# Products of constants in three norms of a two-layer block given up, TensorE waits there

## The reference

```python
def rmsnorm(x, g):
    xf = x.astype(jnp.float32)
    y = xf * lax.rsqrt(jnp.mean(xf * xf, axis=-1, keepdims=True) + EPS)
    return (y * g.astype(jnp.float32)).astype(x.dtype)
...
    for l in range(DEPTH):
        ...
        a_lat = rmsnorm(h, norm1_g[l]) * (1.0 + sc1) + sh1
        a_ctx = rmsnorm(z, norm1_g[l]) * (1.0 + csc1) + csh1
        o_ctx, o_lat = token_mixer(a_ctx, a_lat, ...)
        h = h + g1 * o_lat
        f_lat = rmsnorm(h, norm2_g[l]) * (1.0 + sc2) + sh2
        h = h + g2 * channel_mixer(l, f_lat, ...)
        if need_ctx:      # layer 0 only
            ...           # the same for the context tokens
    return rmsnorm(h, final_g)
```

## Time and profile before

| what | value |
|---|---|
| median of 3 executions | 1991.33 us |
| the profiled execution | 1993.04 us |
| its span, first to last instruction | 1991.3 us |
| TensorE busy | 1949.7 us, 98% of the span |
| TensorE loading weights | 1591.6 us, 80% |
| VectorE busy | 1558.4 us, 78% |
| ScalarE busy | 992.6 us, 50% |
| products of constants (L2246) in the trace | 92 instructions, 27.2 to 992.8 us |
| granted clock of TensorE, mean | 0.995 |

### The profile page before, as it was taken

How to read it: one execution, slowest core, us unless ns; L and a number is a source line. 1 busy time by engine, 2 the same in 40 slices (tenths; PEclk the granted TensorE clock), 3 DMA queues, 4 the chain that set the end, 5 groups by cost and what they waited for, 6 DMA issues and landing times.

```text
span 1991.3 us, 25270 instructions
## 1 busy us (share of the span) xinstructions
PE 1949.7 (98%) x10390; PEld 1591.6 (80%) x10390; DVE 1558.4 (78%) x2043; ACT 992.6 (50%) x935; POOL 0.2 (0%) x4
## 2 busy tenths in 40 slices
PE   6999999999999999999999999999999999999998
PEld 3577876788788878889888888888888888888886
DVE  7898798687746757442688988989889898898987
ACT  3422334232212223212377776777767777777775
POOL 0000000000000000000000000000000000000000
PEclk9999999999999999999999999999999999999999
DMA  9466585335433542685379999999999999899994
GB/s 401 118 232 192 144 289 194 115 120 194 185 149 131 191 149 106 216 202 191 128 303 375 352 377 352 343 374 352 373 343 357 369 356 374 332 364 370 361 370 190
DMA packets 83845, 529.29 MB, mean 266 GB/s; under 512 B 23056, under 2 KB 49552, under 8 KB 52752
## 3 DMA queue, kind: packets, MB, share of 16 engines
q1 hardware_dynamic: 62976, 508.60, 69.5%
q10 hardware_dynamic: 20752, 19.05, 2.8%
HBM read 509.34 MB, written 18.28 MB: 265 GB/s over the span
## 4 chain that ended last, share of the span: by engine, by line
PE 91%; DVE 5%; DMA 2%; ACT 1%; issue 1%; SPq 0%; DVEq 0%; ACTq 0%
PE ps L2741 15%; PE ps L2726 15%; PE ps L2727 15%; PE ps L2151 7%; PE ps L2160 6%; PE ps L2167 6%; PE ps L2164 6%; PE ps L2179 2%; PE ps L2182 2%; PE ps L2185 2%; PE ps L2512 1%; PE ps L2362 1%; PE ps L2655 1%; DMA ring<-in_w_mod 1%; PE ps L2463 1%
## 5 line engine op out<-in xcount | busy, mean ns | idle before, releaser
L1965 DVE TENSOR_TENSOR WL<-mring,WH 128x2048 fp32r<-128x2048 f32 x336 | 755.1, 2287 | 102.2 <-ACT WH L1189 102.0
L1189 ACT ACTIVATE WH<-mring 128x2048 fp32r<-128x2048 f32 x336 | 626.2, 1913 | 136.1 <-PE ps L2741 125.7
L2726 PE MATMUL ps<-WH,XGh 128*128 128x512 f32 x896 | 354.5, 396 | 0.2 <-issue 0.2
L2727 PE MATMUL ps<-WH,XGl 128*128 128x512 f32 x896 | 350.4, 391 | 0.0
L2741 PE MATMUL ps<-WL,XGh 128*128 128x512 f32 x896 | 221.5, 389 | 0.0
L2741 PEld LDWEIGHTS ps<-WL,XGh 128*128 128x128 f32 x896 | 168.2, 188 | 34.9
L2726 PEld LDWEIGHTS ps<-WH,XGh 128*128 128x128 f32 x896 | 168.9, 189 | 33.9 <-issue 0.3
L2727 PEld LDWEIGHTS ps<-WH,XGl 128*128 128x128 f32 x896 | 169.0, 189 | 33.6
L920 ACT ACTIVATE FWH<-ring 128x4096 fp32r<-128x4096 f32 (+2 forms) x21 | 67.6, 3221 | 217.0 <-DMA ring<-in_ffn_gu 127.3
L2726 PE MATMUL ps<-WH,hTh 128*128 128x512 f32 x440 | 172.7, 392 | 0.0
L2727 PE MATMUL ps<-WH,hTl 128*128 128x512 f32 x440 | 171.4, 390 | 0.0
(11 more groups left out here) (422 smaller groups left out, 2703.3 us busy)
## 6 DMA issues: line engine op xcount, KB each, us to landing
mring<-in_moe_gate SPq DMA_DIRECT2D x56, 2048.0 KB, 9.5
mring<-in_moe_up SPq DMA_DIRECT2D x56, 2048.0 KB, 9.7
mring<-in_moe_down SPq DMA_DIRECT2D x56, 2048.0 KB, 9.5
ring<-in_w_mod SPq DMA_DIRECT2D x23, 2048.0 KB, 9.2
ring<-in_w_in SPq DMA_DIRECT2D x11, 2048.0 KB, 8.6
ring<-in_ffn_gu SPq DMA_DIRECT2D x11, 2048.0 KB, 8.0
ring<-cks SPq DMA_DIRECT2D x4, 2048.0 KB, 8.8
ring<-in_w_out SPq DMA_DIRECT2D x4, 2048.0 KB, 8.5
```

Of the source, the lines that this page charges most:

```text
L1189: nc.scalar.activation(WH[buf][:, o], mring[t % MRING][:, o], ACT.Copy).then_inc(high_done, 1)
L1965: V.tensor_tensor(WL[buf][:, o], mring[t % MRING][:, o], WH[buf][:, o].bitcast(F32), ALU.subtract).then_inc(low_done, 1)
L2726: mm(out_, ah, WH[buf][:, o:o + 512], start=(first and q == 0), stop=False)
L2727: mm(out_, al, WH[buf][:, o:o + 512], start=False, stop=False)
```

## The change

The products of constants ahead of `inverse_rows` and behind it go in three of the four norms. The norm ahead of layer 0's mixer keeps its own, and so do the places before the state products, behind the router and behind the ranks. The bank that they used behind a mixer is still waited for; in layer 1's first norm the wait for a bank goes with them, and `split_inputs`, the next but one, waits for the same bank itself.

```diff
@@ -2388,9 +2388,7 @@
                 n_ = NT - t0
                 if l:
                     sums(l, 0)
-                    keep_on(bank_for(pe, ("u", 1, 0)), 3)
                     inverse_rows(l, 0)
-                    keep_on(place(("u", 1, 0))[0], 4)
                 if l == 0:
                     pe.wait_ge(ahead_in[1], 16)
                 else:
@@ -2567,9 +2565,7 @@
                 else:
                     taken(pe, ("out", 1, 5))
                     idle_bank = ps[:, 5, :]
-                keep_on(idle_bank, 3)
                 inverse_rows(l, 1)
-                keep_on(idle_bank, 2 if l else 4)
                 if l == 0:
                     for i_, (name, _, t) in enumerate(ffn_tiles):
                         pe.wait_ge(w_high, i_ + 1)
```

## The result

| | before | changed |
|---|---|---|
| median of 5 executions | 1991.44 us | 2001.15 us |
| lowest and highest | 1989.35, 1995.57 | 2000.45, 2005.54 |
| ratio, 95% interval | 1 | 1.0053 [1.0037, 1.0069] |
| the profiled execution, its span | 1993.04, 1991.3 us | 2000.45, 1998.6 us |

The ratio is worth 10.6 us (7.4 to 13.7). The two profiled executions lie only 7.3 us apart in span. Part of these missing 3 us turned out to matter: the execution of before that was profiled took 1.6 us longer than its median, the one of the changed kernel 0.7 us less.

A forecast was written before the change was run, and what follows sets the result against it. TensorE was taken to bound the kernel (91% of the span's chain of waits). Losses of 1.6 + 1.6 + 2.8 = 6.0 us at three norms, on a median of 1991.33, gave 1997.3 us; range 1993 to 2001.5.

The forecast's parts named there:

- No slack on TensorE, nothing returned by the work taken away: Three norms: TensorE delays reach the end; removing the products returns at most 0.1 us a norm, taken as 0.
- The clock falls behind each of the three norms: Three norms: without the products TensorE idles (23% busy over 5 us at the first) and its granted clock falls.
- Rival 1: Clock holds in the first two norms and falls at the router where it does now: 1991.3 us; chance 0.10.
- rival 2: Only the third norm loses the clock, its lull running through the router: 1994.1 us; chance 0.08.
- The price of a fall ahead of dense products, 1.6 us: First and second norm: one 3.4 us lowered stretch costs 1.6 us each, 3.2 together; bounds 0 and 6.4.
- rival 3: At a norm ahead of dense products, a clock fall lasting two lowered stretches; chance 0.08.
- high price: Upper costs: 3.2 us at a norm ahead of dense products, 4.4 us at the router.
- The third norm, 2.8 us: Router: clock falls about 3.4 us earlier, slowing five quick rounds (2.7 us) and the sixth (0.1); bounds 0 and 4.4.
- Nothing returns there: Behind the router: the ten instructions of constants take 4.06 us at the lower clock again, so no time returns.
- Rival 4: Earlier router fall ends earlier; constants run faster and the fall at 1000.7 us may not come: 1990.6 us; chance 0.04.
- The sum: Whole kernel: 1.6 + 1.6 + 2.8 = 6.0 us longer, median 1997.3 us; chance 0.70.
- The range: Whole kernel: median from 1993 us up to 2001.5, the upper end with two of three terms at their highest cost.

The follow-up runs named there:

- e1: Against the kernel before, only the norm behind layer 0's mixer gives up its products of constants; ratio 1.0019 [1.0008, 1.0029].
- e2: Against the kernel before, only the norm ahead of layer 1's mixer gives up its products of constants; ratio 1.0017 [1.0004, 1.0031].
- e3: Against the kernel before, only the norm behind layer 1's mixer gives up its products of constants; ratio 1.0029 [1.0015, 1.0043].
- e5: Against the kernel before, the three norms keep only the products of constants behind the spreading products; ratio 1.0019 [1.0005, 1.0034].
- e6: Against the kernel before, the three norms keep only the products of constants ahead of the spreading products; ratio 1.0029 [1.0019, 1.0040].
- e10: Kernel before plus two products of constants in the router, behind its third and sixth rounds; ratio 1.0002 [0.9992, 1.0012].
- e7: Kernel before with the three norms' products of constants made 32 columns wide instead of 128, same number and places; ratio 0.9996 [0.9984, 1.0007].

## Why the prediction was right in the mechanism and wrong in the size

**No slack on TensorE, nothing returned by the work taken away.** Right. The way from the spreading products to the next dense one is 3.12 us in both kernels, from C's sums to the router 5.28 and 5.27 us. In the changed kernel's first profile the losses reach the end in full: from the experts' first product to the last norm's sums both kernels take 982.96 us.

**The clock falls behind each of the three norms.** Right, in all profiles of the changed kernel and of e1 to e3: nine norms without products, nine falls. Eight profiles have all products of A, and eight all of B, and none of these shows a fall there. At C the clock can fall with the products too: in three of seven profiles, 3.2 to 4.2 us behind the router's start and for 6.8 us. Without them it falls in all three, 0.4 to 0.8 us behind that start and for 10.2 to 13.7 us. Rival 1 had for it that L2239 parts the wait, and that kept nothing: with idle times of 1.64 and 2.00 us parted by 1.13 us of work the clock stands at 0.53 to 0.74 in the stretches at A and B shown above, and e5 and e6 lose it at B (0.55 and 0.51) with only one of the two. Rivals 1 and 2 are out.

**The price of a fall ahead of dense products, 1.6 us.** Too low on average. Measured at A 2.3, 1.6 and 1.7 us, at B 2.2, 2.8 and 2.2: means of 1.9 and 2.4, together 4.3 where the sum had 3.2. One lowered stretch of 3.4 us costs 1.6 us, as worked out; but in four of the six cases the clock stayed down for 6.8 us. Such a fall of two stretches had 0.08 in the chances, as rival 3, which was too little. In all four it starts before the first dense product, by 0.8 to 2.4 us, so a part of it is free, and it costs 2.2 to 2.8 us. The 3.2 us that the bounds and the range take for a norm at its high price (6.4 for two) are shown by no run. The term of 1.6 us a norm was too small by 0.3 and 0.8 us.

**The third norm, 2.8 us.** Here is the step that failed, with the price just told. The five quick rounds did turn slow, as the prediction said. But it took them from a profile in which the clock had fallen in the sixth round anyway and in which the ten instructions behind had taken 4.06 us, and it carried the difference over to the median of before ("about one lowered stretch" below the profile), as if the router's fall were still in it. An execution of before without the fall needs 17.8 us from router to experts, not 20.1; the changed kernel needs 21.8 to 23.4. Against such an execution the third norm costs 4.0 to 5.5 us up to the experts. All eight rounds are quick in it, 5.04 us from 979.71 to 984.75, where the changed kernel takes 9.21, from 984.13 to 993.34: 4.2 us for the rounds alone, and the rest in the ten instructions and the ranks behind them. "Nothing returns there" was right against that one profile: two more of before have those ten instructions in 2.3 us.

Rival 4 had named what can come back behind that: a fall at the experts that "may not come", worth 1.6 us. It came in the changed kernel's first profile and not in its second nor in e3's, which leaves 2.4 us for C in these two. It can't be put down to the change: before's three profiles have that fall and those of e1, e6 and e10 don't. As a whole rival 4, a faster kernel, is out.

**The sum.** With the means of the profiles it is 1.9 + 2.4 + 4.5 = 8.8 us up to the experts, against an execution with a quiet router; with what came back behind them in two of three, C's mean is 3.4 and the sum 7.7. The two comparisons of the changed kernel gave 10.6 (7.4 to 13.7) and 7.6 (4.8 to 10.2), and the three norms one by one 3.8 + 3.4 + 5.8 = 13.0, each give or take 2 to 3; the standstill near the end, 1.0 + 1.0 + 2.4 = 4.4 us in their profiles, may be what this has too much. Within the intervals the parts are additive; that they are exactly so is not shown. How much of the 4.6 us between 6.0 and 10.6 is due to each term stays open: the two that were too small give 1.1 (A and B) and 0.6 to 1.7 (C) by the means of the profiles, and the rest lies within the interval. The range had a slip too: two of the three at their high price, 3.2 + 3.2 + 2.8 or 3.2 + 1.6 + 4.4, both make 9.2 and 2000.5 us, not 2001.5.

**The spread.** The executions of before spread by 7 us in two comparisons (1987.9 to 1995.1) and by 11 in another (1988.5 to 1999.4). Falls explain a part (2.3 us for one in the router, 1.6 for one behind the experts' first product). Another part lies ahead of A, where 368.9 to 374.0 us pass from the first sums to A's sums, with kernels that don't differ there. The two longest, 373.3 and 374.0 us, are the profiles of e6 and e10; the others lie below 371.5. In these two ScalarE's queue is held for 8.43 and 6.50 us by two DMA issues, which take 1.46 to 3.66 us in the others, and its next instruction, whose result TensorE waits for, comes late. The first row is before's, the other two are e6's, the issues and the wait:

```profile
289.55 2.05 ACTq L861 DMA_DIRECT2D cks<-CWh  x2
288.88 8.43 ACTq L861 DMA_DIRECT2D cks<-CWh  x2
PE ps L2213 <- ACT aT L909: 4.1, 1, 4.1
```

Why the issues take longer in some executions stays open.

## What to carry to other kernels

Products that nobody reads can be worth more than they cost: nineteen of them stood in three norms, over the waits of the first two the clock was at 1.00 in every profile that kept them (eight of each), and giving them up cost 0.4 to 0.5% and returned nothing. Waits of 1.6 and 2.0 us around 1.1 us of work were enough to lose TensorE's clock in six of six cases, and what is lost is half the pace of the dense work behind, while the clock stands at 0.50: 0.43 us a product instead of 0.23. Where the clock falls at a place in some executions and not in others, as it does in the router of before in one profile of three, one profile is one draw: before a term is read from it, hold its time against the median, and look for what that execution has and the median one may not.

## What the runs showed of the hardware that I had not expected

- A product of constants 32 columns wide holds the clock as one of 128 does (e7: 369.98 against 370.00 us on way A, ratio 0.9996).
- The same program at the same norm (A) is lowered for 6.8 us in one execution, beginning 1.8 us before the first dense product, and for 3.4 us in another, beginning 1.0 us behind it. At the router, without C's products, it is down for 10.2 to 13.7 us, from the first or second round of 8-column products and transposes through the last, and comes back 1.8 to 4.8 us after the ten instructions of constants have begun.
- With one of two idle times left (1.6 or 2.0 us), the same profile shows the clock kept at one norm and lost at the next (e5, e6).
- A fall of 3.4 us behind the experts' first product costs 1.6 us and is there in seven of thirteen profiles: in all three of before, in one of the two of the changed kernel.
- Two DMA issues on ScalarE's queue take 1.46 to 3.66 us in eleven profiles and 6.50 and 8.43 us in two, and the products that wait for ScalarE come up to 4.1 us late.
